# The causal mask of the prompt's score blocks: added by VectorE instead of by TensorE products

## The reference

```python
def fox_block(q, k, v, cq, ck, q_pos, k_pos):
    s = jnp.einsum('bqhd,bkhd->bhqk', q, k).astype(jnp.float32) * (HEAD_DIM ** -0.5)
    s = s + jnp.swapaxes(cq, 1, 2)[..., :, None] - jnp.swapaxes(ck, 1, 2)[..., None, :]
    mask = k_pos[None, :] <= q_pos[:, None]
    p = jax.nn.softmax(jnp.where(mask, s, -jnp.inf), axis=-1)
    return jnp.einsum('bhqk,bkhd->bqhd', p.astype(v.dtype), v)
```

## Time and profile before

| what | before |
|---|---|
| median of 3 runs | 1409.5 us (1409.11 to 1409.52) |
| the profiled execution's own time | 1408.32 us |
| its span in the profile | 1406.4 us |
| TensorE (PE) busy | 1369.0 us, 97% of the span |
| VectorE (DVE) busy | 922.0 us, 66% |
| ScalarE (ACT) busy | 636.6 us, 45% |
| GpSimd (POOL) busy | 575.6 us, 41% |
| mean granted TensorE clock | 0.997 of full speed |

### The profile page before, as it was taken

One profiled execution on the slowest core, in us unless ns is written; L12 is line 12 of the kernel. 1 busy time (PEld: TensorE's weight loads), 2 busy tenths in 40 slices (PEclk: granted clock), 3 DMA queues, 4 the chain that ended last, 5 costly groups with the idle time before them and its releaser, 6 DMA issues.

```text
span 1406.4 us, 25060 instructions
## 1 busy us (share of the span) xinstructions
PE 1369.0 (97%) x8382; PEld 1086.1 (77%) x8382; DVE 922.0 (66%) x2025; ACT 636.6 (45%) x1364; POOL 575.6 (41%) x606
## 2 busy tenths in 40 slices
PE   8999999999999999999999999999999999999998
PEld 7999767788877777777777777777777777778886
DVE  3789755593376778666433676776776776497775
ACT  6766423332353354445333455555555655422121
POOL 2122442200033234221100556877977867644452
PEclk9999999999999999999999999999999999999999
DMA  7885699987349769787998767448458355556552
GB/s 234 295 281 199 201 268 252 275 273 228 113 139 272 248 223 266 243 266 237 313 321 264 170 189 158 107 98 181 103 109 181 83 114 196 160 169 199 191 177 89
DMA packets 211023, 284.21 MB, mean 202 GB/s; under 512 B 49809, under 2 KB 146481, under 8 KB 207409
## 3 DMA queue, kind: packets, MB, share of 16 engines
q1 hardware_dynamic: 209856, 282.61, 68.7%
q10 hardware_dynamic: 1040, 0.00, 0.0%
HBM read 191.12 MB, written 90.19 MB: 200 GB/s over the span
## 4 chain that ended last, share of the span: by engine, by line
PE 60%; DVE 3%; POOL 2%; ACT 2%; issue 2%; DMA 2%; SPq 1%; DVEq 0%; ACTq 0%; POOLq 0%
PE in_g L927 14%; PE attn_pv L2531 10%; PE attn_s L2601 6%; PE attn_s L2500 6%; PE attn_s L2505 5%; PE attn_pv L2601 5%; PE attn_s L2485 5%; PE attn_s L2513 2%; PE in_b L1102 1%; POOL in_hv L1810 1%; PE in_b L1054 1%; PE attn_s L2554 1%; PE attn_s L2502 1%; PE in_b L1157 1%; PE in_b L1122 1%
## 5 line engine op out<-in xcount | busy, mean ns | idle before, releaser
L927 PE MATMUL in_g<-in_wh,in_xh 128*128 128x512 f32 (+2 forms) x904 | 331.4, 380 | 6.2 <-ACT in_xh L1219 2.4
L927 PE MATMUL in_g<-in_wl,in_xh 128*128 128x512 f32 (+2 forms) x904 | 321.9, 369 | 0.0
L2807 POOL TENSOR_TENSOR attn_probs<-attn_probs,attn_probs_turned 128x512 f32<-128x512 f32 (+3 forms) x200 | 214.3, 1072 | 64.9 <-ACT attn_probs_turned L2633 40.9
L927 PE MATMUL in_g<-in_wh,in_xl 128*128 128x512 f32 (+2 forms) x904 | 236.4, 380 | 1.4 <-DVE in_xl L1532 1.3
L2847 DVE TENSOR_REDUCE attn_tops<-attn_s 128x1 f32<-128x512 f32 (+3 forms) x288 | 159.1, 596 | 108.6 <-PE attn_s L2485 108.6
L2633 ACT ACTIVATE attn_probs_turned<-attn_s 128x512 f32<-128x512 f32 (+1 forms) x352 | 161.2, 545 | 125.7 <-PE attn_s L2505 124.8
L927 PEld LDWEIGHTS in_g<-in_wh,in_xh 128*128 128x128 f32 x904 | 165.5, 189 | 40.8 <-issue 7.4
L927 PEld LDWEIGHTS in_g<-in_wl,in_xh 128*128 128x128 f32 x904 | 165.6, 189 | 27.9
L927 PEld LDWEIGHTS in_g<-in_wh,in_xl 128*128 128x128 f32 x904 | 159.1, 190 | 34.9 <-issue 5.3
L1808 POOL TENSOR_SCALAR in_hs<-in_hs 128x8 f32<-128x8 f32 (+1 forms) x53 | 19.5, 368 | 401.8 <-DVE in_hs L1559 401.8
L2531 PE MATMUL attn_pv<-attn_probs_turned,attn_v 128*64 128x256 f32 (+1 forms) x1216 | 142.1, 363 | 0.0
(11 more groups left out here) (377 smaller groups left out, 2685.8 us busy)
## 6 DMA issues: line engine op xcount, KB each, us to landing
in_xu<-scratch_xt SPq DMA_DIRECT2D x87, 512.0 KB, 5.4
in_xl<-scratch_xt SPq DMA_DIRECT2D x34, 512.0 KB, 4.6
in_raw<-in_w_in SPq DMA_DIRECT2D x40, 256.0 KB, 5.2
scratch_xt<-in_xu SPq DMA_DIRECT2D x19, 512.0 KB, 4.4
scratch_xt<-in_xl SPq DMA_DIRECT2D x17, 512.0 KB, 5.0
scratch_k<-in_x_turned SPq DMA_DIRECT2D x17, 512.0 KB, 7.2
scratch_q<-in_x_turned SPq DMA_DIRECT2D x17, 512.0 KB, 5.4
in_x_turned<-in_x_prompt SPq DMA_DIRECT2D x16, 512.0 KB, 4.8
```

The source lines that it names most:

```text
L927: last = X.matmul(g_ps[b][:, 0:m], x, ws[:, c, w0:w0 + m], start=(c == 0 and h == 0 and ws is wh), stop=(c == KC - 1 and h == 1))
L2807: E.tensor_tensor(acc[:, part:, :], acc[:, part:, :], mine, ALU.add).then_inc(added[engine], 1)
```

## The change

The product that adds the mask is left out. A second mask, `causal_turned`, is made at the start by GpSimd (a memset and an affine_select more). A step `mask` is put into the list for each diagonal block, behind the cycle's four `scores` and ahead of its four `exp`: VectorE waits for the block's `s_score`, adds the mask to the 128x128 diagonal part in the bank and counts up `s_masked`. The `exp` of such a block waits for `s_masked` in place of `s_score`.

```diff
@@ attention_order
         order += [("scores", b) for b in mine]
+        order += [("mask", b) for b in mine if scores[b][0].kind == "fox" and scores[b][1] >= scores[b][0].first]
         order += [("exp", b) for b in mine]
@@ gpsimd_program
+            G.memset(K.causal_turned[:, :], 0.0).then_inc(s_const, 1)
...
+            G.affine_select(out=K.causal_turned[:, :], in_=K.causal_turned[:, :], compare_op=ALU.is_ge, fill=MASKED,
+                            base=0, pattern=[[1, P]], channel_multiplier=-1).then_inc(s_const, 1)
@@ tensor_steps
                     X.matmul(bank[:, part:, :], y2[h][:, keys], x2[h][:, q], start=True, stop=False)
-                    if u.kind == "fox" and k >= u.first:
-                        X.matmul(bank[:, part, :], causr[:, :], identr[:, :], start=False, stop=False)
@@ scalar_steps
-                    act.wait_ge(s_score, s + 1)
+                    if ("mask", s) in masks:
+                        act.wait_ge(s_masked, masks.index(("mask", s)) + 1)
+                    else:
+                        act.wait_ge(s_score, s + 1)
@@ vector_steps
+                if what == "mask":
+                    u, k, at = scores[s]
+                    block = ring_ps[ring.at["scores", s]][:, at, :]
+                    dve.wait_ge(s_score, s + 1)
+                    V.tensor_tensor(block, block, K.causal_turned[:, :], ALU.add).then_inc(s_masked, 1)
```

More of the change, by code:

```diff
@@ L101 @@
 ROOM = 26624
-CONSTS = 8
+CONSTS = 10
 GATED = {"state": SSM, "memq": MEM, "gate": FOX}
@@ L1784, in gpsimd_program @@
             G.memset(K.causal[:, :], 0.0).then_inc(s_const, 1)
+            G.memset(K.causal_turned[:, :], 0.0).then_inc(s_const, 1)
             G.memset(K.neghalf[:, :], -0.5).then_inc(s_const, 1)
             G.memset(K.one[:, :], 1.0).then_inc(s_const, 1)
-            pool.wait_ge(s_const, 5)
+            pool.wait_ge(s_const, 6)
             for of in (K.ident, K.identb):
@@ L2152, in attention_and_output @@
         s_addp, s_addv, s_den, s_denr, s_rden = (a.sem(k) for k in ("added_p", "added_v", "den", "den_read", "rden"))
+        s_masked, masks = a.sem("masked"), [x for x in order if x[0] == "mask"]
         s_store = [a.sem(f"stored{h}") for h in range(2)]
@@ L3013, in build @@
         D.rows_of = rows_of
-        K.ident, K.identb, K.causal = a.sb("ident", [P, P]), a.sb("identb", [P, P], BF16), a.sb("causal", [P, P], BF16)
+        K.ident, K.identb = a.sb("ident", [P, P]), a.sb("identb", [P, P], BF16)
+        K.causal, K.causal_turned = a.sb("causal", [P, P], BF16), a.sb("causal_turned", [P, P], BF16)
         K.neghalf, K.one = a.sb("neghalf", [P, FOX_HEADS]), a.sb("one", [P, 1])
```

## The result

The changed kernel takes 1418.4 us, median of four runs (1415.9 to 1419.9), against 1409.3 for the kernel before in runs on the same chip: a ratio of 1.0067, 95% interval 1.0048 to 1.0086, so 0.7% slower, some 9 us. The prediction said 1417.0.

What follows compares the result with a forecast made beforehand. TensorE was taken to set the pace, busy 429.75 of 432 us in the attention's stretch. Terms +9.3, -2.0, -0.8, +1.4 and -0.4 gave +7.5 on 1408.3, plus 1.2 for the median: 1417.0 us, range 1409.5 to 1424.

Steps and rivals of the forecast that it cites:

- the ring's slack: In the ring of banks tying ScalarE to TensorE, exps can be about 0.4 us late before TensorE loses time.
- The removed product at 0.11 us: On TensorE, each mask product left out saves 0.11 us: 0.43 per diagonal cycle, 13.8 in 32 if nothing else waits.
- first rival: Exps have more slack, so 24 diagonal cycles gain 0.43 us each, cycles 6 almost nothing: 1398.9 us; 8 in 100.
- The mask at 0.29 us: On VectorE, each 128x128 mask add takes 0.29 us; where VectorE is free, the first exp starts 0.33 us behind its block.
- The rival of 0.54 us for each: Mask adds stretched to 0.54 us make waits in every diagonal cycle, +8 us, 1425 us; 10 in 100.
- The cycle 6: Masks queue behind two reductions and two reciprocals on VectorE: `values` 1.2 us later in seven heads, 0.9 in the last.
- The other diagonal cycles: The 24 with VectorE mostly free: cycles 0 gain 0.25 us, cycles 2 and free cycles 10 0.07, the last 0.4.
- The long adds: In about four cycles 10, a 1.31 us VectorE add ahead of the masks costs 0.35 us each, +1.4 in all.
- The sum: All cycle terms together +7.5 us on the profiled 1408.3; with 1.2 for the median of runs, 1417.0 us, 0.5% slower.
- masks are hidden: The first rival by its title: faster, -10.6 us, 1398.9 us; 8 in 100.
- half of it: Rival: cycles 6 lose only 0.6 us each, giving 1412 us, no change; 15 in 100.
- TensorE's busy time loses its 128 mask rows: Sign expected in the changed profile: TensorE's busy time drops by its 128 mask rows without the span following.

## Why the prediction was right

- **What bounds the kernel, and the ring's slack.** Right. Two kernels with VectorE almost equally loaded, one with the exps waiting and one without, are 19 us apart. The "0.4 us of slack" held as it was meant, with TensorE as late as in the kernel before: exps 0.22 us late cost nothing net in a cycle 2 (-0.08), exps 0.56 late cost 0.70. It is no slack once the products are gone: against no mask anywhere the same cycle loses 0.33.
- **The removed product at 0.11 us, 13.8 us in all "if nothing else waits".** The price was right: 0.11 at the first top (0.42 to 0.45 us for four), 0.10 by the lengths of the cycles 2 and 10. The sum of the removal is 9.3 us, 9.9 with the attention's first cycle (in the trace without mask whose clock did not fall), since the cycles 6 give next to nothing; the text had that in its first rival, with the same second top and den. By the 81 ns for a 128-column matmul in the Trainium skill ("TensorE: Matmul & The Clock Gate", section "Back-to-back issue gap") four products would be an estimated 0.32; the rows do not agree, with 0.42 to 0.45 at the first top.
- **The mask at 0.29 us, never stretched.** Right: 274 to 300 ns, with GpSimd at work beside it. The rival of 0.54 us for each, 10 in 100, fell.
- **The cycle 6.** Right in its rows: first exp at 2.22 (2.32 by the working), releaser VectorE, standstills ahead of the third top, the fourth and the row, `values` at 3.79 (3.8). Predicted +1.2 a head, measured +1.15 to +1.17. Two sizes were off. The last head lost 1.50 in place of 0.9, and 0.26 more in the cycle behind, for a long add (1.54 us) stood ahead of its dens and masks. And one cycle lost 1.5 more to the fallen clock, a term that the sum did not have. Together +11.1 for +9.3.
- **The other diagonal cycles.** Cycles 2 and the free cycles 10 right (-0.08, -0.06 to -0.07). Cycles 0 gave 0.16 to 0.18 in place of 0.25: even with no mask the cycle is only 0.31 to 0.35 shorter, since the exps hold its fourth top. The long adds cost 0.23 in place of 0.35, and three heads had them, not four.
- **The sum.** +7.5 predicted, +9.9 in the attention of the two traces (the mis-sized terms nearly all err to one side: cycles 6 +1.8, cycles 0 +0.7, last cycle +0.5, long adds -0.7), +9.1 between the medians (the two spans are 7.3 apart, since before's execution had come to the attention 2.3 us later). The rivals "masks are hidden" and "half of it" needed the exps of a cycle 6 to start less than 0.6 us late, or its loss to be 0.6; they were 1.35 late and it was 1.15.
- **One sign that did not come.** "TensorE's busy time loses its 128 mask rows": it stayed at 1369.0 us, and in the attention's stretch it rose from 421.97 to 423.53. A busy time of overlapping rows is not a sum of prices. And the time itself came closer than the terms: the timed runs of the changed kernel other than the profiled one took 1417.9 to 1419.9 us at a granted clock of 0.994 to 0.995, the profiled one 1415.9 at 0.997, so part of what separates 1417.0 from 1418.4 is a clock that the sum did not have.

## What to carry to other kernels

Work moved from the engine that sets the pace to one that idles is worth what stands *ahead of it in that engine's queue* at the place where it is wanted: 24 of these 32 cycles were even, and eight lost more than all 32 could give, because two reductions happened to be queued there. Where nothing is queued the new step still has a price (here 0.33 us for a 0.41 us gain). So look up, cycle by cycle, when the helping engine comes to the new step, and when its result is wanted, before counting idle time. And where the pacing engine already waits for something in that cycle (here a den's bank), taking work off it gives nothing.

## What the runs showed of the hardware beside

- A VectorE add of two tiles in SBUF, 128x128, took 273 to 1621 ns, median 880, with GpSimd at work beside it; the add with one operand in PSUM took 274 to 300 ns in 128 cases, and the one-operand maximum in SBUF 256 to 292. Each of the 94 stretched adds started inside a GpSimd instruction and ended 143 to 153 ns after its end. This is how the Trainium skill has it ("SBUF — State Buffer", section "SBUF: two separate sides"): a VectorE instruction with two inputs in SBUF shares a port pair with a GpSimd instruction that reads SBUF, and the one that starts first holds it for its whole instruction while the other waits. The trace agrees for the 94; nine adds took 273 to 294 ns though a GpSimd instruction was under way.
- TensorE's granted clock fell from 2.4 to 1.2 GHz for 3.4 us in a cycle 6, right behind its standstills. Of the seven heads that have them, it fell in one where they were 0.2 to 0.3 and 0.65 us (in the changed kernel's trace; in one of seven too where the masks are in the cycles 6 alone), and in all seven where they were 0.2 to 0.3 and 0.98. Such a stretch added 0.9 to 1.5 us to a wait that was itself 1.1. The longest standstill alone doesn't decide it: with the masks ahead of the second den TensorE stood still once for 0.98 to 1.09 us in each of seven heads, and in the last head of the kernel with the mask twice for 1.85 us, and the clock fell in none of these. What decides is not shown by these runs.
